# The mixer of the second block as one stage of 70 ticks, with the gate projection spread over them

## What is computed

```python
def hybrid_mixer(h, cos, sin, layer_idx, w_in, b_fgt, ..., w_gate, b_gate, w_br_a, w_br_b, w_br_c, w_br_d, w_out):
    aq, ak, av, bq, bk, bv, bf, cq, ck, cv, dq, dk, dv, diq, dik, diw = split(h @ w_in)
    ya = diff_attention(rope(aq), rope(ak), av, lam)          # 4 heads, two softmaxes each
    yb = forgetting_attention(bq, bk, bv, bf + b_fgt)         # 4 heads, bias from a cumulative sum
    yc = stick_breaking_attention(cq, ck, cv)                 # 4 heads, weights from a reversed sum
    yd = indexed_sparse_attention(rope(dq), rope(dk), dv, rope(diq), rope(dik), diw, topk=64)
    g = sigmoid(h @ w_gate + b_gate)                          # (256, 4, 1024): 32 blocks of 128 columns
    merged = g[0] * (ya @ w_br_a) + g[1] * (yb @ w_br_b) + g[2] * (yc @ w_br_c) + g[3] * (yd @ w_br_d)
    return merged @ w_out
```

## Time and profile before

| | |
|---|---|
| median of three runs | 5324.82 us |
| profiled execution, its own time | 5323.69 us |
| its span | 5322.0 us |
| PE busy | 4621.6 us (87%) |
| DVE busy | 3122.0 us (59%) |
| ACT busy | 2266.6 us (43%) |
| mean granted PE clock | 0.917 |

### The profile page before, as it was taken

The page is one execution under the profiler, slowest core; times in us unless marked ns, Lnnn a source line. Parts: engine busy times, 40 slices in busy tenths (PEclk is TensorE's granted clock), DMA queues, the critical chain, the costliest instruction groups (busy, mean ns, idle before and its releaser), DMA issues. The chain is left out here.

```text
span 5322.0 us, 72934 instructions
## 1 busy us (share of the span) xinstructions
PE 4621.6 (87%) x25788; PEld 3882.1 (73%) x25788; DVE 3122.0 (59%) x7266; ACT 2266.6 (43%) x4298; POOL 6.3 (0%) x20
## 2 busy tenths in 40 slices
PE   7768899999999999776899999788858798874978
PEld 2446788888878888545899977578638788862977
DVE  7545688555444444425787677655575555556555
ACT  6423333666533333213448755444324444423444
POOL 0000000000000000000000000000000000000000
PEclk9889999999999999887999999889859899985989
DMA  8400444455656666201566788544204335420343
GB/s 303 151 26 32 141 129 133 163 181 182 208 185 189 190 189 186 72 33 63 179 216 230 262 264 267 187 169 151 81 0 166 146 146 185 149 67 12 154 158 146
DMA packets 355500, 810.27 MB, mean 152 GB/s; under 512 B 29864, under 2 KB 171304, under 8 KB 335508
## 3 DMA queue, kind: packets, MB, share of 16 engines
q1 hardware_dynamic: 355224, 806.79, 45.0%
HBM read 704.87 MB, written 101.81 MB: 152 GB/s over the span
## 5 line engine op out<-in xcount | busy, mean ns | idle before, releaser
L170 DVE TENSOR_TENSOR w_low__6<-w_raw,w_high__6 128x512 fp32r<-128x512 f32 x544 | 362.0, 688 | 440.7 <-ACT w_high__6 L165 440.3
L158 PE MATMUL hidden<-hT_high,w_high__6 128*128 128x512 f32 x1152 | 456.7, 396 | 15.3 <-DVE w_low__6 L170 15.3
L160 PE MATMUL hidden<-hT_high,w_low__6 128*128 128x512 f32 x1152 | 450.8, 391 | 0.0
L159 PE MATMUL hidden<-hT_low,w_high__6 128*128 128x512 f32 x1152 | 449.0, 390 | 0.0
L170 DVE TENSOR_TENSOR w_low__11<-w_raw__2,w_high__11 128x512 fp32r<-128x512 f32 x544 | 362.6, 689 | 122.2 <-ACT w_high__11 L165 106.8
L165 ACT ACTIVATE w_high__6<-w_raw 128x512 fp32r<-128x512 f32 x544 | 324.2, 624 | 216.8 <-PE side L160 204.4
L165 ACT ACTIVATE w_high__11<-w_raw__2 128x512 fp32r<-128x512 f32 x544 | 321.8, 624 | 70.9 <-PE side__2 L160 35.6
L158 PE MATMUL hidden__3<-hT_high__2,w_high__11 128*128 128x256 f32 x1152 | 331.8, 288 | 11.3 <-DVE w_low__11 L170 11.3
L160 PE MATMUL hidden__3<-hT_high__2,w_low__11 128*128 128x256 f32 x1152 | 327.4, 284 | 0.0
L159 PE MATMUL hidden__3<-hT_low__2,w_high__11 128*128 128x256 f32 x1152 | 327.1, 284 | 0.0
L158 PEld LDWEIGHTS hidden<-hT_high,w_high__6 128*128 128x128 f32 x1152 | 217.2, 189 | 58.3 <-DVE w_low__6 L170 15.6
(11 more groups left out here) (1034 smaller groups left out, 12746.1 us busy)
## 6 DMA issues: line engine op xcount, KB each, us to landing
w_raw<-in_peer_u SPq DMA_DIRECT2D x128, 512.0 KB, 3.8
w_raw<-in_peer_v SPq DMA_DIRECT2D x128, 512.0 KB, 3.8
w_raw__2<-in_peer_u SPq DMA_DIRECT2D x128, 512.0 KB, 4.0
w_raw__2<-in_peer_v SPq DMA_DIRECT2D x128, 512.0 KB, 4.9
activated_dram<-activated SPq DMA_DIRECT2D x128, 256.0 KB, 4.1
routing_dram<-routing SPq DMA_DIRECT2D x32, 1024.0 KB, 6.2
routing_chunk<-routing_dram SPq DMA_DIRECT2D x16, 2048.0 KB, 10.7
activated_again<-activated_dram SPq DMA_DIRECT2D x128, 256.0 KB, 4.1
```

The source lines that it names most:

```text
L158: nc.tensor.matmul(out, lhs[0], rhs[0], start=start, stop=False, skip_group_check=True)
L159: nc.tensor.matmul(out, lhs[0], rhs[1], start=False, stop=False, skip_group_check=True)
L160: return nc.tensor.matmul(out, lhs[1], rhs[0], start=False, stop=stop, skip_group_check=True)
L170: return nc.vector.tensor_tensor(low, src, high.bitcast(F32), ALU.subtract)
```

## The change

`mixer_vectors`, `rotate`, `index_bias`, `stick_probs` and `attention` go, and one stage `mixer_chain` takes their place. All its engines step through the same 70 ticks: 17 for the rotation (ticks 0 to 16, with the work of `mixer_vectors` in between), 8 for the index scores (17 to 24), 10 for the top 64 and the stick weights (25 to 34), 32 + 3 for attention (35 to 69). In each of the ticks 0 to 63 stands half a block of the gate projection: 12 products on PE (`gate_half`), a high part on ACT and a low part on DVE for the half four ticks ahead, and in every second tick a finished block is moved from its bank (`keep_gate`). SP stores each block to DRAM (`gates_dram`). `gated_merge` reads the gates from there and has the branch products alone. The input's split is made once, in a stage of its own (`split_cols`), and `project_cols` and `project_rows` take it as `parts`. Other differences: the ReLU of the index scores is on ACT now, for both query tiles at once; stick work is per head, 512 columns wide; attention has three score banks and one output bank, and DVE waits for its own writes once for all that a tick has written (`Lazy`) instead of once for each (`Chain`).

```diff
-def project_cols(nc, w, nblocks, kc, src, n, dst, ring):
+def project_cols(nc, w, nblocks, kc, src, n, dst, ring, parts=None):
...
+        s_high, s_low = parts or [st.sbuf(x, [P, kc, n], F32R) for x in ("src_high", "src_low")]
...
-            pe.wait_ge(src_split, kc)
+            if not parts:
+                pe.wait_ge(src_split, kc)
...
-            with pe.Fori(0, KC) as n:
-                for b, (lo, hi) in enumerate(chunks):
-                    pe.wait_ge(split[b], n + 3)
-                    pe.wait_ge(gated[b], n + 1)
-                    for c in range(KC):
-                        cut = slice(c * P, (c + 1) * P)
-                        three_products(nc, psg[b][:, 0:T], (high[:, b, cut], low[:, b, cut]),
-                                       (h_parts[0][:, c, :], h_parts[1][:, c, :]), c == 0, c == KC - 1)
-                    for c in range(lo, hi):
-                        cut = slice(G + (c - lo) * P, G + (c - lo + 1) * P)
-                        last = three_products(nc, psb[b][:, 0:T], (high[:, b, cut], low[:, b, cut]),
-                                              (y_parts[0][:, c, :], y_parts[1][:, c, :]), c == lo, c == hi - 1)
-                    last.then_inc(ready[b], 1)
...
+def mixer_chain(nc, ident, consts, cols, w, l, hT, h_parts, cos, sin, qk, vals, sticks, ya, yT, gates_dram):
...
+        NR = len(turned_blocks)
+        IDX_AT = NR
+        TOP_AT = IDX_AT + 8
+        ATT_AT = TOP_AT + 10
+        TICKS = ATT_AT + U + 3
+        HALVES = 2 * NB * KC
...
+            sp.dma_start(pick[:, :], consts["sel4"]).then_inc(landed[4], 16)
+            for b in range(1, NB * KC + 3):
+                if b < NB * KC:
+                    if b >= RR:
+                        sp.wait_ge(split, 2 * (b - RR + 1))
+                    sp.dma_start(raw[:, b % RR, :], weights(b)).then_inc(w_loaded[b % RR], 16)
+                d = b - 3
+                if d >= 0:
+                    sp.wait_ge(gate_kept, d + 1)
+                    sp.dma_start(gates_dram[d], gate[:, d % GR, :]).then_inc(gate_stored[d % GR], 16)
+            for r in range(GR):
+                sp.wait_ge(gate_stored[r], 16 * len(range(r, NB * KC, GR)))
...
+            def gate_half(n):
+                b, half = n // 2, n % 2
+                pe.wait_ge(split, n + 1)
+                if half == 0 and b >= 2:
+                    pe.wait_ge(gate_kept, b - 1)
+                for c in range(half * KC // 2, (half + 1) * KC // 2):
+                    cut = slice(c * P, (c + 1) * P)
+                    last = three_products(nc, psg[b % 2][:, 0:T], (high[:, b % RB, cut], low[:, b % RB, cut]),
+                                          (h_high[:, c, :], h_low[:, c, :]), c == 0, c == KC - 1)
+                last.then_inc(used, 1)
...
+            def index_dots(m):
+                a = 64 * (m % 2)
+                if m == 0:
+                    pe.wait_ge(rotated, NR)
+                    pe.wait_ge(fox_ready, 1)
+                if m >= 3:
+                    pe.wait_ge(rel_ready, m - 2)
+                for t in range(TT):
+                    last = nc.tensor.matmul(ps[(0, 1, 4)[m % 3]][:, t * T:(t + 1) * T],
+                                            qk[a:a + 64, BLK["iq"] + m // 2, t * P:(t + 1) * P],
+                                            qk[a:a + 64, BLK["ik"], :], start=True, stop=True)
+                last.then_inc(dots, 1)
...
+            for k in range(TICKS):
+                if k == 7:
+                    spread()
+                if k < NR:
+                    swap(k)
+                if IDX_AT <= k < IDX_AT + 8:
+                    index_dots(k - IDX_AT)
+                    if k >= IDX_AT + 4:
+                        stick_scores(k - IDX_AT - 4)
+                if k >= ATT_AT:
+                    attend(k - ATT_AT)
+                if k < HALVES:
+                    gate_half(k)
+
+        @block.scalar
+        def _(act):
+            def make_high(n):
+                b, half = n // 2, n % 2
+                cut = slice(half * 512, (half + 1) * 512)
+                if half == 0:
+                    act.wait_ge(w_loaded[b % RR], 16 * (b // RR + 1))
+                if b >= RB:
+                    act.wait_ge(used, n - 2 * RB + 1)
+                high_part(nc, high[:, b % RB, cut], raw[:, b % RR, cut]).then_inc(high_ready, 1)
+
+            def keep_gate(b):
+                act.wait_ge(used, 2 * b + 2)
+                if b >= GR:
+                    act.wait_ge(gate_stored[b % GR], 16 * (b // GR))
+                at = b % NB * KC + b // NB
+                nc.scalar.activation(gate[:, b % GR, :], psg[b % 2][:, 0:T], ACT.Identity, bias=gate_b[:, at:at + 1]) \
+                    .then_inc(gate_kept, 1)
+
...
+            for k in range(TICKS):
...
+                if k >= ATT_AT:
+                    attend(k - ATT_AT)
+                if k + AHEAD < HALVES:
+                    make_high(k + AHEAD)
+                if k % 2 == 0 and 2 <= k <= HALVES:
+                    keep_gate(k // 2 - 1)
+        @block.vector
+        def _(dve):
+            chain = Lazy(dve, own)
+
+            def make_low(n):
+                b, half = n // 2, n % 2
+                cut = slice(half * 512, (half + 1) * 512)
+                dve.wait_ge(high_ready, n + 1)
+                low_part(nc, low[:, b % RB, cut], raw[:, b % RR, cut], high[:, b % RB, cut]).then_inc(split, 1)
...
+                if i < U:
+                    nk = units[i]["nk"]
+                    for j, (_, _, bias, _) in enumerate(units[i]["parts"]):
+                        m = first[i] + j
+                        r = m % SS
+                        dve.wait_ge(scores_ready, m + 1)
+                        if m >= SS:
+                            dve.wait_ge(exp_done, m - SS + 1)
+                        chain.wrote(nc.vector.scalar_tensor_tensor(logits[:, r, 0:nk], ps[r][:, 0:nk], scale, bias,
+                                                                   ALU.mult, ALU.add))
+                before_units = 0 <= i - 1 < U
+                if before_units:
+                    for j in range(len(units[i - 1]["parts"])):
+                        m = first[i - 1] + j
+                        r = m % SS
+                        dve.wait_ge(exp_done, m + 1)
+                        chain.wrote(nc.vector.reciprocal(inv[:, 0, r:r + 1], total[:, r:r + 1]))
+                chain.settle()
+                if i < U:
+                    for j in range(len(units[i]["parts"])):
+                        r = (first[i] + j) % SS
+                        nc.vector.tensor_reduce(nmax[:, r:r + 1], logits[:, r, 0:nk], X, ALU.max, negate=True) \
+                            .then_inc(max_ready, 1)
...
+            for k in range(TICKS):
+                if k < NR:
+                    rotate_first(k)
...
+                if k >= ATT_AT:
+                    attend(k - ATT_AT)
+                if k + AHEAD < HALVES:
+                    make_low(k + AHEAD)
+            chain.settle()
+            dve.wait_ge(out_kept, U)
...
-def gated_merge(nc, gate_w, branch_w, gate_b, hT, yT, mergedT):
+def gated_merge(nc, branch_w, gates_dram, yT, mergedT):
...
+        @block.sync
+        def _(sp):
+            for n in range(KC):
+                if n >= 2:
+                    sp.wait_ge(split, n - 1)
+                sp.dma_start(raw[:, n % 2, :], branch_w[n]).then_inc(w_loaded[n % 2], 16)
+                if n >= GR:
+                    sp.wait_ge(opened, n - GR + 1)
+                sp.dma_start(logit[:, n % GR], gates_dram[NB * n:NB * (n + 1)].rearrange("b p t -> p b t")) \
+                    .then_inc(gate_loaded[n % GR], 16)
+
+        @block.tensor
+        def _(pe):
+            for n in range(KC):
+                pe.wait_ge(split, n + 1)
+                for b, (lo, hi) in enumerate(chunks):
+                    if n == 0:
+                        pe.wait_ge(y_split, hi)
+                    if n >= 2:
+                        pe.wait_ge(gated, NB * (n - 2) + b + 1)
+                    for c in range(lo, hi):
+                        cut = slice(c * P, (c + 1) * P)
+                        last = three_products(nc, psb[n % 2][b][:, 0:T], (high[:, n % 2, cut], low[:, n % 2, cut]),
+                                              (y_high[:, c, :], y_low[:, c, :]), c == lo, c == hi - 1)
+                    last.then_inc(used, 1)
...
+            for n in range(KC):
+                if n + 1 < KC:
+                    make_high(n + 1)
+                act.wait_ge(gate_loaded[n % GR], 16 * (n // GR + 1))
+                if n >= 2:
+                    act.wait_ge(gated, NB * (n - 1))
+                nc.scalar.activation(g[:, n % 2], logit[:, n % GR], ACT.Sigmoid).then_inc(opened, 1)
...
+            def add(n):
+                dve.wait_ge(gated, NB * (n + 1))
+                for pair in range(2):
+                    last = nc.vector.tensor_tensor(prod[:, n % 2, 2 * pair, :], prod[:, n % 2, 2 * pair, :],
```

(52 more changed lines are left out.)

726 lines of the change are left out of this document (405 added, 321 removed).

## The result

The changed kernel takes 5233.62 us as the median of four runs (5228.72 to 5234.47), the kernel before 5326.90 in the same comparison: a ratio of 0.982 with a 95% interval of 0.981 to 0.983, 93 us less (1.8%). A second series on another occasion gave 5228.59 us and 0.982 (0.981 to 0.983). The forecast was 5221 us, with a range of 5165 to 5295.

The account below looks back on a forecast made before the run. Bound: one long stretch by small steps, on DVE above all, with PE cold; the merge by PE. Chain +41, merge -96, split +3 make -52 a layer, -104 for both: 5221 us as a median, range 5165 to 5295.

Parts of the forecast that it names:

- the circle: Gate blocks: load waits for store, store for keep_gate, that for high part, that for the load before; 4.9 us per two ticks.
- Opening and rotation: Chain's start and its 17 rotation ticks: 14.4 us until index weights are ready, then 48 us, bounds 36 and 61.
- the rival without a circle: Rotation, attention and merge: loads land in time, PE and DVE set ticks; 26 us less a layer, 5169 us; chance 11%.
- Index: Eight index-score ticks: PE sets them, 2.44 us each, 3.44 in the last four with stick scores; 25 us.
- The rival of drains: Half-height scores around gate halves: tiling-mode changes drain TensorE, 0.3 us in 44 ticks, +13 a layer, 5247 us; chance 5%.
- Top 64: Ten ticks of top-64 rounds and stick work: only DVE counts, with ten low parts; 41 us.
- Attention: 35 attention ticks, 29 with a gate half: 89 us, where 63.4 were before.
- Merge: gated_merge with 240 products left: DVE sets 4.0 us an output block; 44 us against 139.7, bounds 40 and 55.
- Split: Own stage splitting the input: 2.77 us plus a stage border, first weights landing later, 1 us given back; +3 a layer.
- longer loads: Gate-weight loads: 4.7 us a load makes 6.4 us per two ticks, 25 us more a layer, 5271 us; chance 15%.
- Hand-offs: Attention: waits between PE and DVE cost 1 us in 28 ticks, +28 a layer, 5277 us; chance 14%.
- PE did not stay cold: Denies a rival for the chain: PE cold throughout, chain 299 us, +46 a layer, 5416 us, slower than before; chance 5%.

Follow-up runs that it names:

- opening the circle: Changed kernel with each finished gate block stored one step later, so a load stands behind the store five blocks before, not four: 5216.19 us, ratio 0.980.
- all edits together: Changed kernel plus later stores, split in project_cols, forget bias on ACT, index-tick halves moved, keep_gate earlier, row halves alternating, half before transposes: 5172.47 us, ratio 0.971.

## Why the prediction came out as it did

The mechanism was right: most of the gate products went into ticks that left PE idle, and the circle that was foreseen was there. The sum was 8 us too favourable: 104 forecast, 96 found in the stages. Part of the closeness is luck, since terms of the chain erred against each other.

- *Opening and rotation*: 62.4 forecast, 57.5 found in the first layer and about 62 in the second, by its longer opening. Two terms erred against each other. The turn of the circle was 5.5 us, not 4.9. But the vectors' work and the circle were added, though DVE does the one while it waits for the other, and the four halves made ahead spare the first ticks a wait. Failed step: "about half of it fits into DVE's slack of 0.65 a tick, so +4". With the circle closed nearly all of it fits; with it open nothing does, and the 39.8 us come from DVE. That is why the rival without a circle (5169) was far off as well: 26 a layer forecast, 6 to 7 found.
- *Index*: 25 forecast, 26.3 and, at a clock of 1.00, 23.5 found. The ticks are 2.67 and 3.53 us instead of 2.44 and 3.44. A product took less than the 0.5 that was put down, 0.43 (4746.81 to 4747.24), but each change between half-height and full-height products costs about 0.2. From the last gate product before the scores to the second behind them pass 2.36 us (4746.06 to 4748.42); four products at 0.43 and two steps of 0.12 are 1.96, so 0.4 is left. A full-height swap in the same place leaves nothing: 0.67 us (3850.05 to 3850.72, with the bias on ACT) against 0.43 and twice 0.12.

```profile
3850.05 0.28 PE L160 MATMUL gate<-hT_high__4,gate_w_low 128*128 128x256 f32 x1
3850.17 0.59 PE L2040 MATMUL chain<-qk,swap 128*128 128x256 f32 x2
3850.41 0.47 PE L158 MATMUL gate<-hT_high__4,gate_w_high 128*128 128x256 f32 x1
3850.72 0.28 PE L159 MATMUL gate<-hT_low__4,gate_w_high 128*128 128x256 f32 x1
```

  The rival of drains had 0.3 a tick; the index ticks show 0.4, which the 0.5 for a product had half covered.
- *Top 64*: 41 forecast, 41.5 found, DVE busy for 97% of it.
- *Attention*: 89 forecast, 94.9 found. The sixteen units over 128 keys took 46 us, not 41, again the circle (5.5 us a pair from 3962.89 to 3990.56; with it open they take 41). The four with two softmaxes over 256 keys took 4.0 us each, not 3.4. The failed step is "The units with two softmaxes are DVE's": PE was busy for 13.87 of 15.99 us and DVE for 12.68, and PE waited besides.

```profile
3990.56:4006.55 15.99, 13.87 (x82) 9.83 (x82) 12.68 (x42) 8.36 (x26) 0.00 (x0) 1.00 0.28 84
PEld chain L2073 <- ACT exps__2 L2153: 2.3, 3, 0.8
PEld chain L2087 <- DVE probs__2 L2374: 2.1, 3, 1.4
```

  The second score and its wait for a bank were left out of PE's side of the sum, which took the 1.58 us of a unit with one softmax. What holds these units at 4.0 us stays open: without the transposes' wait they took as long.
- *Merge*: 44 forecast, 43.6 and 42.0 found, for the reason given.
- *Split*: 3 forecast, 3.7 found.
- *The rivals*: longer loads came true in part (4.2 us, between 3.2 and 4.7 of the earlier trace rows); the whole circle costs some 7 us a layer, 5 of them in attention. Hand-offs stayed small: putting the half ahead of the transposes gave 2 us a layer. PE did not stay cold.

That the second layer's chain part is 2 to 3 us longer with the same code lies in its opening, which takes 3.5 to 4.4 us more at the lower granted clock shown above; the first layer of the profiled execution had lost 3 us by the clock in its index ticks. What stays open: why the clock falls in one and not in the other, and why the work ahead of the second block varies by up to 13 us between runs.

## What to carry to other kernels

Work that is spread over the ticks of a latency-bound stage costs what the bounding engine of each tick pays for it, so place it by that: here a half costs some 1.5 us where PE sets the tick (12 us for the eight of the index ticks) and 0.5 where DVE does (5 us for the ten of the top-64 ticks). Moving ten halves accordingly gave 14 us over both layers, opening the circle as much. Follow a queue that holds both loads and stores in written order: a load behind a store that waits for the load's own product makes a circle as long as the latency. And a circle can hide other work that is just as long; here removing it gave the rotation 0 to 2 us, and moving that work then gave 7.

Compare stages, not totals, when a change is worth a few microseconds, and read the granted clock of each stage beside its length: the same instructions took 3 us more or less by it here.

## What the hardware showed beyond the expectation

A 512 KB load took 3.7 us as a median with no stores in the ticks, and 4.2 us with a 128 KB store just ahead of it in the queue. Products of 64 rows on different row halves started in the same instant, and four took 1.06 instead of 1.92 us. A stay among half-height products between full-height ones cost 0.4 us. With an index stage that ran at once behind warm products, PE kept a clock of 1.00 for 10 us of half-height products alone, where the kernel before ran its own at half clock. With all edits together the same ticks had a mean of 0.83.
